# Activations stored with even and odd tokens apart, and read by TensorE from the two parts in turn

## What is computed

```python
def reference(x, meta_tokens, ...):
    h = jnp.concatenate([meta, x], axis=1)
    for i in range(DEPTH):
        j = i // 2
        hn = _rms(h, norm_mix[i])
        if i % 2 == 0:
            h = h + _even_mixer(hn, ab_w_in[j], ..., ab_w_out[j])
        else:
            h = h + _odd_mixer(hn, c_w_in[j], ..., c_w_out[j])
        h = h + _conv_ffn(_rms(h, norm_ffn[i]), ffn_w_up[i], ffn_conv_w[i], ffn_conv_b[i], ffn_w_down[i])
    return h[:, N_META:]

def _conv_ffn(h, w_up, conv_w, conv_b, w_down):
    u = h @ w_up
    ...
    g, val = jnp.split(acc, 2, axis=-1)
    return (jax.nn.silu(g) * val) @ w_down
```

## Time and profile before

| | |
|---|---|
| median of 3 runs | 2572.63 us (2571.23 to 2573.11) |
| the profiled execution, its own time | 2570.12 us |
| its span, first to last instruction | 2568.4 us |
| mean granted TensorE clock | 0.997 |
| busy: PE, PEld | 98%, 95% |
| busy: DVE, ACT, POOL | 65%, 47%, 6% |
| read from HBM | 416.31 MB, 163 GB/s over the span |

### The profile page before, as it was taken

One profiled execution on the slowest core, in us unless ns is written; L12 is line 12 of the kernel. 1 busy time (PEld: TensorE's weight loads), 2 busy tenths in 40 slices (PEclk: granted clock), 3 DMA queues, 4 the chain that ended last, 5 costly groups with the idle time before them and its releaser, 6 DMA issues.

```text
span 2568.4 us, 50438 instructions
## 1 busy us (share of the span) xinstructions
PE 2529.5 (98%) x19301; PEld 2432.8 (95%) x19301; DVE 1672.4 (65%) x2301; ACT 1198.2 (47%) x1540; POOL 152.8 (6%) x186
## 2 busy tenths in 40 slices
PE   8999999999999999999999899999999999999999
PEld 6998998999999999999999888999999899989998
DVE  5446796576655665566565777576767667666674
ACT  4344645454433444344358545444544444434443
POOL 0000011200000000000000456100000000000000
PEclk9999999999999999999999999999999999999999
DMA  6544455555555555555555333456565555565654
GB/s 179 173 138 124 125 149 127 168 164 171 178 179 168 174 171 176 167 188 170 173 164 150 109 92 99 125 180 194 167 196 180 189 181 175 186 192 176 194 182 154
DMA packets 430508, 420.25 MB, mean 164 GB/s; under 512 B 26066, under 2 KB 428284, under 8 KB 430364
## 3 DMA queue, kind: packets, MB, share of 16 engines
q1 hardware_dynamic: 416448, 415.29, 51.8%
q10 hardware_dynamic: 13932, 3.17, 1.1%
HBM read 416.31 MB, written 2.10 MB: 163 GB/s over the span
## 4 chain that ended last, share of the span: by engine, by line
PE 87%; DVE 6%; ACT 3%; issue 2%; ACTq 1%; POOL 1%; DMA 0%; DVEq 0%
PE ps L1408 27%; PE ps L1406 24%; PE ps L1407 24%; PE ps L1404 6%; DVE w_lo L916 2%; PE ps L1629 2%; ACT w_hi L536 1%; PE ps L1474 1%; PE ps L1473 1%; PE ps L1454 1%; DVE gl_e L1249 0%; DVE rt L1113 0%; DVE rt L1121 0%; PE ps L1475 0%; PE ps L1621 0%
## 5 line engine op out<-in xcount | busy, mean ns | idle before, releaser
L1406 PE MATMUL ps<-act_hi,w_hi 128*128 128x272 f32 (+1 forms) x4864 | 1410.7, 290 | 5.5 <-DVE w_lo L916 5.5
L1407 PE MATMUL ps<-act_lo,w_hi 128*128 128x272 f32 (+1 forms) x4864 | 1392.4, 286 | 0.0
L1408 PE MATMUL ps<-act_hi,w_lo 128*128 128x272 f32 (+1 forms) x4864 | 1391.2, 286 | 0.0
L916 DVE TENSOR_TENSOR w_lo<-raw,w_hi 128x1024 fp32r<-128x1024 f32 (+1 forms) x800 | 951.3, 1205 | 575.4 <-ACT w_hi L536 552.3
L536 ACT ACTIVATE w_hi<-raw 128x1024 fp32r<-128x1024 f32 (+1 forms) x797 | 819.5, 1038 | 787.2 <-PE ps L1408 765.7
L1406 PEld LDWEIGHTS ps<-act_hi,w_hi 128*128 128x128 f32 x4864 | 917.3, 189 | 13.3 <-issue 9.0
L1407 PEld LDWEIGHTS ps<-act_lo,w_hi 128*128 128x128 f32 x4864 | 918.3, 189 | 1.5
L1408 PEld LDWEIGHTS ps<-act_hi,w_lo 128*128 128x128 f32 x4864 | 917.9, 189 | 0.0
L1408 PE MATMUL ps<-g_both,w_lo 128*128 128x272 f32 (+1 forms) x1408 | 400.9, 285 | 0.0
L1408 PEld LDWEIGHTS ps<-g_both,w_lo 128*128 128x128 f32 x1408 | 265.2, 188 | 0.0
L1404 PE MATMUL ps<-g_both,w_hi 128*128 128x512 f32 x704 | 247.3, 395 | 0.0
(11 more groups left out here) (241 smaller groups left out, 1325.2 us busy)
## 6 DMA issues: line engine op xcount, KB each, us to landing
raw<-in_ffn_w_up SPq DMA_DIRECT2D x352, 512.0 KB, 4.6
raw<-in_ffn_w_down SPq DMA_DIRECT2D x128, 512.0 KB, 3.5
raw<-in_ab_w_in SPq DMA_DIRECT2D x96, 512.0 KB, 3.7
raw<-in_c_w_in SPq DMA_DIRECT2D x96, 512.0 KB, 3.7
raw<-in_ffn_w_down SPq DMA_DIRECT2D x64, 384.0 KB, 3.7
raw<-in_ab_w_out SPq DMA_DIRECT2D x32, 512.0 KB, 3.4
raw<-in_c_w_out SPq DMA_DIRECT2D x32, 512.0 KB, 4.3
tok<-in_x SPq DMA_DIRECT2D x4, 512.0 KB, 7.9
```

Of the source, the lines that this page charges most:

```text
L916: V.tensor_tensor(w_lo[:, s % 4, 0:kc * 256], raw[:, s % 4, 0:kc * 256], w_hi[:, s % 4, 0:kc * 256].bitcast(F32), ALU.subtract).then_inc(S ...
L1406: mm(o, wh, xh[:, kk, t0:T], start=(c == 0 and k == 0), stop=False)
L1407: mm(o, wh, xl[:, kk, t0:T], start=False, stop=False)
L1408: ins = mm(o, wl, xh[:, kk, t0:T], start=False, stop=end)
```

## The change

The tokens of each tile of `act_hi`, `act_lo` and `g_both` are stored as two parts, the 136 even ones and then the 136 odd ones. A helper `parted` makes a view of a row of tokens that runs over the even tokens first and then over the odd ones. Every copy and subtraction that fills these tensors reads its source through it and writes the parts; the readers of `act_hi` and `g_hi` among them see the parted order too. Every product reads its moving columns through a view that takes a token from the even part, one from the odd part, and so on, so that the columns reach TensorE, and PSUM, in the old order of tokens. The number of columns of each product and the sizes of the tensors stay as they were. In the built program the moving operand of a 272-column product was `[1, 272]` (step, count) and is `[1, 136], [136, 2]`; that of the wide product was `[272, 2], [1, 256]` and is `[272, 2], [1, 128], [136, 2]`. The source of a splitting copy was `[1, 272]` and is `[1, 2], [2, 136]`; its result is still a plain run of 272. The sequence of instructions, of their waits and of their tiles is the same on every engine as before.

```diff
-        act_hi = sb("act_hi", [P, KT, T], F32R)
-        act_lo = sb("act_lo", [P, KT, T], F32R)
+        act_hi = sb("act_hi", [P, KT, 2, T // 2], F32R)
+        act_lo = sb("act_lo", [P, KT, 2, T // 2], F32R)
...
-        g_both = sb("g_both", [P, MT, 2, T], F32R, at=zone)
-        g_hi, g_lo = g_both[:, :, 0, :], g_both[:, :, 1, :]
+        g_both = sb("g_both", [P, MT, 2, 2, T // 2], F32R, at=zone)
+        g_hi, g_lo = g_both[:, :, 0, :, :], g_both[:, :, 1, :, :]
...
+        def parted(ap):
+
+            dims = [list(v) for v in ap.ap]
+            step, n = dims.pop()
+            return bass.AP(ap.tensor, ap.offset, dims + [[step, 2], [2 * step, n // 2]])
...
-                A(act_hi[:, k, :], h[:, k, :], ACT.Copy, scale=vec[:, v0 + k:v0 + k + 1]).then_inc(S("x_hi"), 1)
+                A(act_hi[:, k, :, :], parted(h[:, k, :]), ACT.Copy, scale=vec[:, v0 + k:v0 + k + 1]).then_inc(S("x_hi"), 1)
...
-                    high.append(chain.mark(V.tensor_copy(g_hi[:, bass.ds(i * 2 + m, 1), o0:T], gp[:, m:m + 1, o0:T])))
+                    high.append(chain.mark(V.tensor_copy(g_hi[:, bass.ds(i * 2 + m, 1), :, o0 // 2:], parted(gp[:, m:m + 1, o0:T]))))
...
-                    ins = V.tensor_tensor(g_lo[:, k, o0:T], gp[:, m:m + 1, o0:T], g_hi[:, k, o0:T].bitcast(F32), ALU.subtract)
+                    ins = V.tensor_tensor(g_lo[:, k, :, o0 // 2:], parted(gp[:, m:m + 1, o0:T]),
+                                          g_hi[:, k, :, o0 // 2:].bitcast(F32), ALU.subtract)
...
-                V.scalar_tensor_tensor(act_lo[:, k, :], h[:, k, :], vec[:, v0 + k:v0 + k + 1], act_hi[:, k, :].bitcast(F32),
+                V.scalar_tensor_tensor(act_lo[:, k, :, :], parted(h[:, k, :]), vec[:, v0 + k:v0 + k + 1], act_hi[:, k, :, :].bitcast(F32),
...
+                def moving(x_, kk):
+
+                    return x_[:, kk, :, t0 // 2:].rearrange("p a b -> p b a")
...
-                                    mm(o2, wh, g_both[:, kk, :, t0:T], start=(c == 0 and k == 0), stop=False)
+                                    mm(o2, wh, g_both[:, kk, :, :, t0 // 2:].rearrange("p c a b -> p c b a"), start=(c == 0 and k == 0), stop=False)
                                 else:
-                                    mm(o, wh, xh[:, kk, t0:T], start=(c == 0 and k == 0), stop=False)
-                                    mm(o, wh, xl[:, kk, t0:T], start=False, stop=False)
-                                ins = mm(o, wl, xh[:, kk, t0:T], start=False, stop=end)
+                                    mm(o, wh, moving(xh, kk), start=(c == 0 and k == 0), stop=False)
+                                    mm(o, wh, moving(xl, kk), start=False, stop=False)
+                                ins = mm(o, wl, moving(xh, kk), start=False, stop=end)
```

More of the change, by code:

```diff
@@ L757, in even @@
                         act.wait_ge(S("na_stored"), hd + 1)
-                        A(act_hi[:, 8 + hd, :], ntmp[:, hd % 4, :], ACT.Copy).then_inc(S("x_hi"), 1)
+                        A(act_hi[:, 8 + hd, :, :], parted(ntmp[:, hd % 4, :]), ACT.Copy).then_inc(S("x_hi"), 1)
                     n = at_tick(t, NA0 + 1, 1, NA_UNITS)
@@ L770, in even @@
                         act.wait_ge(S("ml_made"), k + 1)
-                        A(act_hi[:, k, :], y_ml[:, k, :], ACT.Copy).then_inc(S("x_hi"), 1)
+                        A(act_hi[:, k, :, :], parted(y_ml[:, k, :]), ACT.Copy).then_inc(S("x_hi"), 1)
                     yield
@@ L871, in high @@
                 act.wait_ge(S("used"), 8 * (G["gl_out0"]["it0"] - 1) + 5 + k // 4)
-                A(act_hi[:, k, Q0:T], o_tile(k)[:, Q0:T], ACT.Copy).then_inc(S("x_hi"), 1)
+                A(act_hi[:, k, :, Q0 // 2:], parted(o_tile(k)[:, Q0:T]), ACT.Copy).then_inc(S("x_hi"), 1)
             decay = decays()
@@ L1155, in low @@
                 dve.wait_ge(S("x_hi"), 24 + hd + 1)
-                V.tensor_tensor(act_lo[:, 8 + hd, :], ntmp[:, hd % 4, :], act_hi[:, 8 + hd, :].bitcast(F32),
+                V.tensor_tensor(act_lo[:, 8 + hd, :, :], parted(ntmp[:, hd % 4, :]), act_hi[:, 8 + hd, :, :].bitcast(F32),
                                 ALU.subtract).then_inc(S("act_ready"), 1)
@@ L1210, in even @@
                         dve.wait_ge(S("x_hi"), KT + k + 1)
-                        V.tensor_tensor(act_lo[:, k, :], y_ml[:, k, :], act_hi[:, k, :].bitcast(F32),
+                        V.tensor_tensor(act_lo[:, k, :, :], parted(y_ml[:, k, :]), act_hi[:, k, :, :].bitcast(F32),
                                         ALU.subtract).then_inc(S("act_ready"), 1)
@@ L1317, in low_gla @@
                 dve.wait_ge(S("x_hi"), 64 + k + 1)
-                V.tensor_tensor(act_lo[:, k, Q0:T], o_tile(k)[:, Q0:T], act_hi[:, k, Q0:T].bitcast(F32),
+                V.tensor_tensor(act_lo[:, k, :, Q0 // 2:], parted(o_tile(k)[:, Q0:T]), act_hi[:, k, :, Q0 // 2:].bitcast(F32),
                                 ALU.subtract).then_inc(S("act_ready"), 1)
```

## The result

The changed kernel takes 2430.64 us (median of 4 runs, 2428.04 to 2434.12) against 2571.93 us of the kernel before: a ratio of 0.945, 95% interval 0.944 to 0.947. It is 5.5% faster. What came is the second rival, which had 2390 us.

A forecast was written before the change was run, and what follows sets the result against it. TensorE was taken as the bound, products times spacing. The profiled 2570.1 us plus 1868.8 for half-rate reading minus 20 of hidden idle time gave 4418.9; with 2.5 us for the median, 4421, said as 4420 us; range 2560 to 4650 us.

The forecast's parts named there:

- The bound and the sum before: TensorE, whole kernel: number of products times spacing, 2296.7 us of the 2568.4 us span.
- (c): TensorE's 38.9 us idle at mixers, norms and first data: slower products hide about half, 20 us less.
- (a): Moving operand of all 18112 products, read in pairs: one column per 1.2 GHz tick, 1868.8 us more.
- rival 2: Product reads: two places in turn avoid SBUF collisions, 115 ns per 272 columns, 183 us gain, 2390 us; chance 0.10.
- rival 1: Product reads: the reader doesn't care about the pattern, only the copies' cost remains, 2570 to 2580 us; chance 0.24.
- (b): Splitting copies on ScalarE and VectorE: nothing to 0.08 us each, cast up to 0.14 (12 us); taken as 0 on path.

The follow-up runs named there:

- f4: Changed kernel, parted storage kept, but 272-column and wide products read straight on, 258-column ones still in pairs: 2529.93 us, ratio 0.983 to the kernel before.
- f5: Against the kernel with plain storage and only reading order changed: 272-column products read four parts in turn, not two: 2690.62 us, ratio 1.046 to the kernel before.
- f1: Against the kernel before: only act_lo stored in two parts and read in pairs, one of each three products: 2544.95 us, ratio 0.990.

## Why the prediction was wrong

**The bound and the sum before: right.** The number of products times their spacing is what the time hangs on (the sum is some 4 us low, since the 8448 products that read `act_hi` and `act_lo` had 125.8 ns and not 125.3); the 2296.7 us of products in it moved by the change of the spacing and the rest moved by the 23 us that (c) below accounts for.

**The step that failed is the choice of a price in (a).** I bounded it from below by 115 ns a product, taken from the plain float32 pass, and that bound is what was measured: 115.5 ns. I chose instead 226.7 ns, the spacing at half clock, and with it 215.0 and 640.0 ns for the other forms. That these are the prices of pairs was my estimate, and no run shows it: at a granted clock of 1.00 the three took 115.5, 111.4 and 326.1 ns. About half the rate came with other readings, a step of 4 elements of float32r (247 ns) or 8 bytes of bfloat16 (241 ns). What I lacked is that float32r columns come in as if by two ports, so that the two columns of a pair don't have to lie in the same 16 bytes: two ports are inferred from the times, that pairs cost 116 ns is measured. By the same token the run of before was not at the full rate: of its 12 ns above columns / 2.4 GHz pairs took away 10, six of which the rule above explains as changes of 16 bytes. I had this difference as rival 2 at 0.10. Its price, 183 us for 2390, was high in two ways: the products saved 163 us, since those of 258 columns came to 111.4 ns and not 109.1 and the wide pair to 326.1 and not 324.6, and all of it was put on the path.

**The argument against rival 2 was the wrong one.** I said that a plain float32 pass reads neighbours too and has no such 10 ns. It doesn't compare: a plain float32 record takes 229 ns for its 272 columns, 0.84 ns each, so by the rule above its port has twice the time for each (a step of 2 costs it only 240 ns against 229). The row that would have helped is the spacing itself. At 1.2 GHz the run costs 226.7 ns, 272 / 1.2 exactly, at 2.4 GHz 125.3, 12 ns above 272 / 2.4. That fits something with a pace of its own, a little slower than the array at 2.4 GHz; I read the first half as rival 1's evidence and left the second standing.

**(b), the copies: right in size, on the low side.** Of the changed kernel, groups by form: the subtraction and the cast of the feed-forward's middle, and ScalarE's rounding at the norms.

```profile
L982 DVE TENSOR_TENSOR g_both<-gp,g_both 128x272 f32 x36 | 14.2, 438 | 0.0
...
L978 DVE CAST g_both<-gp 128x272 f32 x36 | 9.7, 298 | 0.0
```

```profile
L595 ACT ACTIVATE act_hi<-h,vec 128x272 fp32r<-128x272 f32 x64 | 31.1, 547 | 11.4 <-DVE h L1330 7.0 <-PE ps L1419 4.2
```

The cast of 272 elements takes 298 ns, as the earlier trace rows with 300, so the 12 us of the upper bound are 0. ScalarE's copy at the norms rose from 510 ns to 547, 0.04 us, within the 0.08, and its other three splitting copies by 23 to 36 ns. The subtraction didn't move (438 ns against 437).

**(c) has the right mechanism and here the other sign.** A faster stream leaves less cover for the mixers and norms, so part of the gain comes back as waiting. By the spacings, 10560 x 9.8 + 6144 x 7.1 + 704 x 22.5 ns = 162.9 us should have gone; the span is 139.6 us shorter. TensorE's idle time is 2428.8 - 2373.0 = 55.8 us and was 38.9. The mean granted clock fell from 0.997 to 0.992. The stretch below, beside a mixer, is one place where it did:

```profile
262.00:268.00 6.00, 4.43 (x35) 3.87 (x34) 5.76 (x15) 2.02 (x4) 0.00 (x0) 1.00 0.36 106
268.60:275.40 6.80, 6.80 (x18) 4.18 (x19) 4.95 (x14) 2.65 (x6) 0.00 (x0) 0.50 0.40 114
```

TensorE was busy for 4.43 of 6 us, and then the granted clock fell to 0.50, the 1.2 GHz level, for 6.8 us. The kernel before reached the same products at 275 us. TensorE was busy for 5.90 of the 6 us up to 281 us, and the 18 products then took 3.8 us at a granted clock of 1.00:

```profile
280.90:284.70 3.80, 3.80 (x19) 2.54 (x19) 2.13 (x5) 1.74 (x5) 0.00 (x0) 1.00 0.45 135
```

In all, the changed kernel has eight stretches at 0.50 while it works, 34.0 us together, and the kernel before three, 17.0 us. At 272 columns a product took 226.7 ns there against 115.5, so a microsecond there costs about half of one, and the 17.0 us more some 8.5 us. With the idle time's 16.9 us it makes 25.4, where 23.3 us are to be explained. The kernels with other readings show the same exchange, in both directions (the changes from f4 and f5 are differences of medians, the other two of spans):

| kernel | by the spacings | measured | TensorE idle | at 0.50 |
|---|---|---|---|---|
| before to changed | -162.9 us | -139.6 us | 38.9 to 55.8 us | 17.0 to 34.0 us |
| before to low product in pairs (f1) | -30 | -25.0 | 38.9 to 43.8 | 17.0 to 20.4 |
| changed to straight reading (f4) | +118.8 | +99.3 | 55.8 to 40.2 | 34.0 to 23.8 |
| changed to four in turn (f5) | +306 | +260 | 55.8 to 24.2 | 34.0 to 13.6 |

In all four 83 to 86% of a change of the products' time shows in the whole. That is the other 46 us by which f5 fell short of the 327 us that I had put on the path.

## What to carry to other kernels

Before a wide or unusual reading of the moving operand is judged, compare the spacing of products in a steady stretch with columns / 2.4 GHz. Here the surplus of 12 ns was gone at 1.2 GHz (226.7 ns), it was the reading, and it was worth more than all of TensorE's idle time. For float32r of 256 columns and more, read two rows in turn (`[1, n/2], [d, 2]`; every d tried at 272 columns, from 2 to 1024, gave 116 or 117 ns). For bfloat16 and plain float32 leave runs alone: the same change costs 26% (float32) and 123% (bfloat16). The order can be had by the access pattern alone, with the columns put back during evacuation; no copy need change. Count on some 85% of what the spacings promise.

## What the runs showed of the hardware

- The times of streams from SBUF into TensorE fit a price of about 1.755 ns for each change of 16 bytes, moving columns and weights alike: bfloat16 with 4, 2 and 1 columns in 16 bytes cost 121, 241 and 480 ns for 272 columns, weights with one in 16 bytes 233 to 242 ns for 128. The price was the same at granted clocks of 0.50 and 1.00.
- float32r behaves as if its even and odd columns came by separate streams (a rule fitted to the times): 116 ns in pairs, 125 in a run, 243 at step 2, 122 in pairs with step 2.
- At a granted clock of 0.50 the run isn't slowed: 226.7 ns. By the rule the streams bring a column of a run every 0.44 ns, and a product took 0.83 ns a column there.
- Products of 192 to 258 columns in pairs, one behind the other, cost 111.4 to 111.7 ns whatever their columns.
- The run's last 4 ns, the floor of 111.5 ns, the milder price of alternating between two far places, and the dearer neighbours of a lone pair product at 258 columns are open.
